# Attention scores issued inside the GLA stage, activation-table loads moved behind the norms, and twenty extra matrix products in two norms

## The reference, cut to what matters

```
for l in (0, 1):
    mod  = silu(c) @ w_mod[l] + b_mod[l]                  # 6 * D values for each of two token kinds
    h    = rmsnorm(x) * (1 + sc1) + sh1                   # "norm 0" (l = 0), "norm 2" (l = 1)
    proj = h @ w_in[l]                                    # q, k, v, GLA and convolution inputs
    y    = concat(window_attention, gla, short_conv) @ w_out[l]
    x    = x + g1 * y
    h    = rmsnorm(x) * (1 + sc2) + sh2                   # "norm 1" (l = 0), "norm 3" (l = 1)
    x    = x + g2 * (swiglu(h) if l == 0 else top-2-of-8 experts(h))
out = rmsnorm(x)
```

## Time and profile before

| what | value |
|---|---|
| median of 3 runs | 1474.74 us (1473.89 to 1475.73) |
| the profiled execution | 1467.95 us, of which its span 1466.1 us |
| PE busy | 1306.1 us, 89% of the span |
| DVE busy | 808.1 us, 55% |
| ACT busy | 691.9 us, 47% |
| POOL busy | 97.2 us, 7% |
| mean granted PE clock | 0.95 of full |

### The profile page before, as it was taken

How to read it: one execution, slowest core, us unless ns; L and a number is a source line. 1 busy time by engine, 2 the same in 40 slices (tenths; PEclk the granted TensorE clock), 3 DMA queues, 4 the chain that set the end, 5 groups by cost and what they waited for, 6 DMA issues and landing times.

```text
span 1466.1 us, 19538 instructions
## 1 busy us (share of the span) xinstructions
PE 1306.1 (89%) x7072; PEld 1016.7 (69%) x7072; DVE 808.1 (55%) x1167; ACT 691.9 (47%) x989; POOL 97.2 (7%) x83
## 2 busy tenths in 40 slices
PE   5899987789899999999989957685999999999993
PEld 2576754457688888888869823373888888888873
DVE  2221387753523332333343584753888988898882
ACT  5322253552522212223253442552777787787771
POOL 2200000002011100111200000020000000000001
PEclk9999989799999999999989979897999999999997
DMA  8776325003133312233213549055899999999982
GB/s 308 288 259 226 101 76 198 1 1 101 58 101 104 123 63 84 91 107 119 72 33 126 173 154 326 23 191 187 298 348 371 387 360 352 370 385 358 354 339 101
DMA packets 96735, 282.78 MB, mean 193 GB/s; under 512 B 8720, under 2 KB 10272, under 8 KB 96416
## 3 DMA queue, kind: packets, MB, share of 16 engines
q1 hardware_dynamic: 90880, 264.27, 50.3%
q0 software_dynamic: 3488, 12.06, 2.3%
q10 hardware_dynamic: 2304, 5.58, 1.0%
HBM read 271.39 MB, written 10.49 MB: 192 GB/s over the span
## 4 chain that ended last, share of the span: by engine, by line
PE 78%; DVE 10%; ACT 5%; DMA 4%; issue 3%; SPq 0%; POOL 0%; POOLq 0%; ACTq 0%; DVEq 0%
PE ps L673 13%; PE ps L674 13%; PE ps L675 13%; PE ps L1057 5%; PE ps L1059 5%; PE ps L1058 5%; PE ps L1071 3%; PE ps L1073 3%; PE ps L1075 3%; DMA raw<-in_w_mod 2%; PE ps L650 2%; PE ps L754 2%; PE ps L756 2%; PE ps L755 2%; DVE wlo L568 1%
## 5 line engine op out<-in xcount | busy, mean ns | idle before, releaser
L568 DVE TENSOR_TENSOR wlo<-raw,whi 128x1024 fp32r<-128x1024 f32 (+2 forms) x271 | 349.3, 1302 | 303.5 <-ACT whi L563 302.5
L563 ACT ACTIVATE whi<-raw 128x1024 fp32r<-128x1024 f32 (+2 forms) x271 | 298.4, 1107 | 225.2 <-PE ps L675 148.4
L673 PE MATMUL ps<-hhi,whi 128*128 128x512 f32 (+1 forms) x736 | 278.8, 379 | 17.8 <-DVE hlo L1631 16.7
L674 PE MATMUL ps<-hlo,whi 128*128 128x512 f32 (+1 forms) x736 | 275.2, 374 | 0.0
L675 PE MATMUL ps<-hhi,wlo 128*128 128x512 f32 (+1 forms) x736 | 275.0, 374 | 0.0
L673 PEld LDWEIGHTS ps<-hhi,whi 128*128 128x128 f32 x736 | 140.4, 191 | 57.5 <-issue 27.1
L675 PEld LDWEIGHTS ps<-hhi,wlo 128*128 128x128 f32 x736 | 140.2, 191 | 26.8
L674 PEld LDWEIGHTS ps<-hlo,whi 128*128 128x128 f32 x736 | 140.6, 191 | 26.1
L568 DVE TENSOR_TENSOR xlo<-raw,xhi 128x1024 fp32r<-128x1024 f32 (+1 forms) x98 | 131.8, 1351 | 19.4 <-ACT xhi L563 17.3
L563 ACT ACTIVATE xhi<-raw 128x1024 fp32r<-128x1024 f32 (+1 forms) x98 | 113.3, 1164 | 44.2 <-PE ps L1075 33.2
L1057 PE MATMUL ps<-whi,hs_hi 128*128 128x512 f32 (+1 forms) x256 | 96.5, 377 | 2.5 <-DVE hs_lo L1964 2.5
(11 more groups left out here) (278 smaller groups left out, 2051.5 us busy)
## 6 DMA issues: line engine op xcount, KB each, us to landing
raw<-in_w_gu SPq DMA_DIRECT2D x230, 512.0 KB, 5.4
raw<-in_w_dn SPq DMA_DIRECT2D x80, 704.0 KB, 8.3
raw<-in_w_mod SPq DMA_DIRECT2D x56, 512.0 KB, 4.8
mraw<-in_w_mod SPq DMA_DIRECT2D x40, 512.0 KB, 4.8
raw<-in_w_fm SPq DMA_DIRECT2D x32, 512.0 KB, 3.6
raw<-in_w_out SPq DMA_DIRECT2D x16, 512.0 KB, 4.2
raw<-in_w_tg SPq DMA_DIRECT2D x8, 512.0 KB, 4.2
y_rows<-back POOLq DMA_DIRECT2D x1, 4096.0 KB, 15.5
```

The source lines that it names most:

```text
L563: nc.scalar.activation(high(v)[:, 0:cols], src[:, 0:cols], ACT.Copy).then_inc(hi_ready, 1)
L568: nc.vector.tensor_tensor(low(v)[:, 0:cols], landed_in(v)[0][:, 0:cols], high(v)[:, 0:cols].bitcast(F32), ALU.subtract).then_inc(lo_ready, 1)
L673: nc.tensor.matmul(outp, whs, xh, start=first, stop=False)
L674: nc.tensor.matmul(outp, whs, xl, start=False, stop=False)
```

## The change

Five edits:

1. **Start.** Pair 3 moves from `raw` to `mraw`, and pair 7 from `mraw` to `raw`, behind the first two projection units. Pair 5 is consumed after `k` = 0, pairs 6 and 7 after `k` = 1, and the transposes of the last group come after `k` = 2.
2. **Seam, both layers.** PE issues the scores of steps 0 and 1 directly after GLA's last output, ahead of the last modulation transposes and of the transposes of `y`. DVE takes the maxima of step 0 after the gating and ahead of the head norm, and those of step 1 behind `y`. ACT makes the probabilities of step 0 before it converts `y`, and those of step 1 between `y` and the convolution part. `mixed` moves behind the first normalising.
3. **Table loads.** The load of the Silu set moves from ahead of the gain and shift to behind the last of them in norms 0, 1 and 2. In norm 3 it goes; a load of that set ahead of the experts was there already and stays.
4. **Products in two norms.** Behind the sums of norms 1 and 2, PE multiplies the next weight unit's high part with itself, twenty times, into bank 7, which nobody reads.
5. The scores and maxima become functions of their own, so that both stages can call them.

```
-        early = pairs(START_PAIRS // 2, MODT // 2)
+        early = pairs(3, START_PAIRS - 1) + pairs(START_PAIRS, MODT // 2)
-        stream0 = pairs(0, START_PAIRS // 2) + proj0 + late0
+        stream0 = pairs(0, 3) + proj0[:2] + pairs(START_PAIRS - 1, START_PAIRS) + proj0[2:] + late0
...
             def start_mods(k):
-                if 1 <= k <= START_PAIRS // 2 - 1:
-                    mod_pair(START_PAIRS // 2 + k)
-                if k == START_PAIRS // 2 - 1:
+                if k == 0:
+                    mod_pair(5)
+                if k == 1:
+                    mod_pair(6)
+                    mod_pair(7)
+                if k == 2:
                     mod_turns(M0 // 4)
...
+            def keep_busy(v, times):
+                pe.wait_ge(lo_ready, v + 1)
+                for _n in range(times):
+                    nc.tensor.matmul(ps[:, 7, :], whi[:, v % H, 0:P], whi[:, v % H, 0:512], start=True, stop=True)
...
             # PE, end of gla(l)
+                pe.wait_ge(rope_ready[l], AT + 1)
+                pe.wait_ge(am_ready[l], n_at)
+                scores(l, 0)
+                pe.wait_ge(o_out[l], n_o)
+                scores(l, 1)
                 mod_turns((PAIR_GLA[l] + GLA_PAIRS[l]) // 2)
-                pe.wait_ge(o_out[l], n_o)
                 pe.wait_ge(y_ready[l], 1)
...
             out_projection(0)
+            keep_busy(V_FFN[0], 20)
             ffn(0, V_FFN[0], 2)
             norm_sum(2)
+            keep_busy(V_PROJ[1], 20)
             projection(1)
...
             # ACT, end of gla(l)
                 nc.scalar.activation(gss[:, 0:n8], gss[:, 0:n8], ACT.Exp, scale=-0.5).then_inc(grs_ready[l], 1)
+                exps(l, 0)
                 act.wait_ge(yT_done, GT * (l + 1))
                 ... # hhi of y
+                exps(l, 1)
                 act.wait_ge(conv_out, 2 * l + 2)
                 ... # hhi of the convolution part
...
             # ACT, out_projection(l)
                 norm_scale(2 * l + 1)
-                nc.scalar.preload_act_table_set("silu_and_others")
                 norm_hi(2 * l + 1)
+                if l == 0:
+                    nc.scalar.preload_act_table_set("silu_and_others")
...
             # ACT, main: norm 0 and norm 2
             norm_scale(0)
-            nc.scalar.preload_act_table_set("silu_and_others")
...
             norm_hi(0, KT // 2, KT)
+            nc.scalar.preload_act_table_set("silu_and_others")
...
             norm_scale(2)
+            norm_hi(2)
             nc.scalar.preload_act_table_set("silu_and_others")
-            norm_hi(2)
...
             # DVE, end of gla(l)
                 o4 = go[:, t0:NTT, :]
+                maxima(l, 0)
                 mods_in((PAIR_GLA[l] + GLA_PAIRS[l]) // 2)
                 ... # head norm, y
+                maxima(l, 1)
...
             # DVE, attention(l)
-                for i in range(len(todo) + 5):
+                for i in range(1, len(todo) + 5):
+                    if 2 <= i < len(todo):
+                        maxima(l, i)
                     ... # normalising of step i - 1
+                    if i == 1:
+                        for f in range(2 * GT):
+                            mixed(f)
```

More of the change, by code:

```diff
@@ L893, in gla, with scores @@
                     mm.then_inc(yT_done, 1)
+            def scores(l, i):
+                t, j = steps(l)[i]
+                if i >= 2:
+                    pe.wait_ge(p_ready[l], 2 * (i - 1))
+                for kv in range(2):
+                    rows = slice(HD * kv, HD * (kv + 1))
+                    nc.tensor.matmul(ps[:, 2 * (i % 2) + kv, 0:keys(t) * P], aq[rows, j, t * P:(t + 1) * P],
+                                     ak[rows, 0:keys(t) * P], start=True, stop=True).then_inc(s_done[l], 1)
             def attention(l):
                 todo = steps(l)
[L897 to L906, removed]
                 def turn(i):
@@ L937, in pv @@
                                 mm.then_inc(pv_done[l], 1)
-                for i in range(len(todo) + 3):
+                for i in range(2, len(todo) + 3):
                     if i < len(todo):
-                        scores(i)
+                        scores(l, i)
                     if 2 <= i < len(todo) + 2:
@@ L1324, in gla, with exps @@
                                          ).then_inc(mixhi[l], 1)
+            def exps(l, i):
+                t, j = steps(l)[i]
+                act.wait_ge(negm_ready[l], i + 1)
+                if i >= 2:
+                    act.wait_ge(pT_done[l], 2 * (i - 1))
+                for kv in range(2):
+                    c = 2 * i + kv
+                    nc.scalar.activation(prob[:, i % 2, kv, 0:keys(t) * P],
+                                         ps[:, 2 * (i % 2) + kv, 0:keys(t) * P], ACT.Exp,
+                                         bias=negm[:, c:c + 1], scale=HD ** -0.5,
+                                         accum_out=psumrow[:, c:c + 1]).then_inc(p_ready[l], 1)
+                act.wait_ge(snk_ready, step0(l) + i + 1)
+                nc.scalar.activation(esink[:, 2 * i:2 * i + 2], snk[:, 2 * i:2 * i + 2], ACT.Exp
+                                     ).then_inc(esk_ready[l], 1)
             def attention(l):
@@ L1343, in turned_out @@
                                              ).then_inc(pT_out[l], 1)
[L1345 removed]
+                for i in range(2, len(todo) + 5):
                     if i < len(todo):
[L1347 to L1350, removed]
[L1351 to L1359 removed]
+                        exps(l, i)
                     if 2 <= i < len(todo) + 2:
```

43 lines of the change are left out of this document (15 added, 28 removed).

## The result

The changed kernel takes 1461.51 us in the median of 4 executions (1460.80 to 1467.11), beside 1474.68 us for the kernel before, measured beside it (4 executions). The ratio is 0.9915 with a 95% interval of 0.9891 to 0.9939: 12.5 us faster, within 9.0 to 16.1. The forecast was 1459.8 us, with a range of 1454 to 1466.

What follows compares the result with a forecast made beforehand. PE was taken as the bound, with 78% of the path, gains coming only where it waits or runs at 1.2 GHz. Terms 2.7 + 3.0 + 1.6 + 2.4 + 3.0 + 0.9 + 1.3 = 14.9 gave 1474.74 − 14.9 = 1459.8 us; range 1454 to 1466.

Steps and rivals of the forecast that it cites:

- Start: Start of the kernel: the second half of norm 0 begins at about 40.2, not 42.88; 2.7 us, bounds 0.2 and 4.04.
- Seams: Between GLA and attention: DVE's idle time before the maxima goes; 3.0 us per layer, bounds 0.8 to 3.96 and 3.34.
- upper bound of 3.34: Layer 1's seam: DVE's idle time before the attention, the most that could be gained there, in us.
- Norms: Norms 1, 2, 3: moved table loads, plus twenty products holding PE's clock in norms 1 and 2; 1.6, 2.4, 0.9 us.
- Gates: Expert gates: the Exp finds its table set loaded, saving the full 1.3 us; 0 if the gather waits for stored rows.
- A, clock not held: Norms 1 and 2: the twenty products fail to hold PE's clock; 1462.7 us, at worst 1466.0; chance 0.12.
- B, the router keeps the clock: Router in norm 3: its shorter hole, 3.3 us, keeps PE's clock, another 3.0 us gained; 1456.8 us; chance 0.14.
- C, PE bounds the first steps at 1.2 GHz: First attention steps: PE at the lower clock leaves 0.8 us of gain per seam; 1464.2 us; chance 0.12.
- D, repeated relapses: Attention loop: out of step, the clock alternates, each relapse costing up to 2.6 us; 1480.6 or 1496 us; chance 0.04.
- The sum: Whole kernel: start, both seams, norms 1 to 3 and gates add to 14.9 us.
- the offset of 6.8 us: Profiled execution of the kernel before, 1467.95, lay 6.8 us below the runs' median; that difference was carried over.

Runs made afterwards that it cites:

- after: The trace of the changed kernel's profiled execution, with all five edits against the kernel before: 1467.11 us; the kernel's median is 1461.51 us.
- the start alone: The kernel before with only the start's order of pairs and their consumption changed: median 1473.43 us, ratio 0.9996 (0.9977 to 1.0016).
- the seam alone: The kernel before with only the seam between GLA (gated linear attention) and attention changed, in both layers: median 1468.19 us, ratio 0.9968 (0.9952 to 0.9984).
- the table loads alone: The kernel before with only the table loads moved: median 1472.19 us, ratio 0.9995 (0.9977 to 1.0012).
- the changed kernel again: The changed kernel measured a second time with no edit: median 1462.15 us, ratio to the kernel before 0.9908 (0.9879 to 0.9937).

## Why the prediction was right

**Start: 2.7 forecast.** From the start of the span, the copy of the third tile comes at 57.7 to 60.1 us in the five traces with the old order (mean 59.2) and at 54.3 to 57.6 in the nine with the new one (mean 56.2): 3.0 us. The second half of the norm starts at 39.39 in after and at 38.6 to 41.0 in the nine (forecast 40.2), and PE's wait for it is 2.63 us and not 4.04. What the prediction did not see is that this gain can be lost at once: GLA 0 became 3.7 us longer. It asserted that behind each edit PE is the bound again and that all that follows merely shifts; GLA 0 is no such stage. PE waits there for DVE, as at the 3.16 us above, and what the clock costs depends on where its low stretches fall. That is the assumption that failed. In all seven traces with the new start and no products in the GLA the stage took the long form, 77.6 to 77.9 us, which is more than the start had gained. The median of the start alone, −0.8 us, has an interval of −3.4 to +2.4, so how much is lost on average stays open.

**Seams: 3.0 each.** The steps were right: `y` at 260.49 (forecast 260.8), the wait for the convolution's rounding, step 2 at 267.01 (267.5), which is 3.13 us nearer to the GLA's end. Layer 0 kept 2.9 us of it in the kernel with the seam alone. Layer 1 gave 3.7 and not 3.0; step 2 came 3.4 us earlier there, and the next two steps 3.7 and 3.5. The upper bound of 3.34, the idle time that goes, was passed. As single differences these have their scatter too: untouched, the attention of layer 0 takes 76.3 us in two traces and 78.2 in two.

**Norms: 1.6, 2.4, 0.9.** Measured 1.57, 2.33 and 1.07. (With its own terms the second comes to 2.5: 763.6 + 2.3 is 765.9, against 768.38.) The first two repeat on the side of after within 0.05 us; without products they scatter by 0.3 to 0.6 where nothing is edited. In norm 3 the part that the load decides is firm: the router starts 3.33 us behind the Ln and not 4.14, 0.8 us less, in every trace. The rest of the 1.07 is the clock's: the same norm took 12.70 us in the start alone, where nothing of it was edited. The sizes came from counting instructions at full clock, and the one assumption in them, that twenty products hold it, was the thing to bet on.

**Gates: 1.3.** The Exp came 1.33 us earlier, the gathered rows 0.2 us later. The size was that of the lower bound, 0 if the gather waits for the stored rows. It did wait for them, but that is not all: in the table loads alone the gather started 1.05 us sooner and landed no sooner, with the DMA engines full. So this is a term that failed, and the step that failed is that the gathered rows hang on the gates. The trace of before could have told a part: its second store went out at 1005.62, between the five loads from 1004.56 on, and its gather came at 1013.79, 8.17 us behind that store, as in after (8.21); and the loads from 1012.03 on hang on the gates too. As to the load itself, 1.33 us is what the Exp gained, which is the row's 1.28 and not the 2.66 us a switch by the Trainium skill (ScalarE: Activation LUTs, "What ACT_TABLE_LOAD costs").

**The rivals.** *A, clock not held:* wrong, it is 1.00 in both norms, in all nine traces that have the products. *B, the router keeps the clock:* wrong; the first group took 1.02 us, and the 3.36 us hole needed its own products (1.3 to 2.7 us, where B had priced 3.0). *C, PE bounds the first steps at 1.2 GHz:* right in the mechanism, in part in the price. In the trace of after one step in layer 0 has transposes of 1.70 us and products of 1.98 us and makes DVE wait 2.44 us, where before the wait for scores at that step was 0.83. That step is not why the attention is 1.6 us shorter and not 2.9, since the seam alone has the same wait (2.53) and keeps 2.9; after loses the difference at the attention's end, where its clock falls once more (0.72 from 314 to 320 us). In layer 1 nothing of the kind happened in this trace, but in that of the changed kernel again DVE waits 2.12 us there and the attention takes 1.4 us longer. *D, repeated relapses:* no trace shows the loop out of step; two or three falls of the clock in the attention of layer 0 are the most, and before has them too.

**The sum** was 14.9 us. By the medians the change gave 13.2 us and, measured a second time, 14.5; by the ratio 12.5, with 9.0 to 16.1. Missing are the 1.3 of the gates and some or all of the start; layer 1's seam gave 0.7 more. That it came out this near is in part luck: the terms that failed, 1.3 and up to 2.7 us, are each smaller than half the width of that interval, 3.5. That the offset of 6.8 us between the profiled execution and the median carries over was wrong for this trace, which came out 5.6 above its median, and right for the median.

Whether transposes count for the clock (the Trainium skill, TensorE: Matmul & The Clock Gate, "Part 4: PE-mode transpose", says that they don't) no run here shows: none had transposes alone in a stretch.

## What to carry to other kernels

Where PE pauses for a few microseconds in a chain of norms, products with something that is ready, put into the pause, cost nothing here and brought 1.0 and 1.9 us in norms 1 and 2 and 1.3 to 2.7 in norm 3: the work behind the pause runs at full clock, and its length no longer scatters. Price the wait behind the one you take away before you count its gain, and ask which transfers the earlier engine will start. And compare two traces by distances between fixed instructions, stage by stage, since a single pair of spans can hide 12 us; then look at the same stage in several traces, since a stage whose clock falls can differ by 2 us without an edit.

## What was not expected of the hardware

A single execution scatters by more than most of these edits are worth: over 59 executions on two chips, the kernel before took 1466.81 to 1483.99 us, with a standard deviation of 3.6. Executions with a lower mean granted clock are the longer ones (0.941 in the longest, 0.950 in the shortest). A store of 512 KB that was issued among five loads of 512 KB released its reader 8.2 us after its issue (7.1 to 9.2 in the seven traces in which the reader waited for it), and landed within 2.7 us without them. A gather that started 1.05 us sooner landed no sooner while the DMA engines were full. Products of 256 columns in the GLA's pauses raised the mean clock of the profiled execution from 0.954 to 0.968, and GLA 0 at full clock is only 0.2 us shorter than in the trace of before at 0.88.
